# Routing three token tiles in one chain, and another order around the first experts

## The chip, the cores and the metric

One core of a Trainium2 chip runs the whole program. The metric is the device time of one execution in microseconds; lower is better. Engines are named as in the profile: PE (TensorE), DVE (VectorE), ACT (ScalarE), POOL (GpSimd) and SP, whose queue issues nearly all DMAs.

## The reference

One layer of a hybrid trunk for 128 context and 256 latent tokens, 384 in all, D = 1024, float32. Four token mixers and a merge come first and are not touched. Then comes the mixture of experts, of which this case is:

```python
h = modulated RMSNorm(x)                      # (384, 1024)
scores = sigmoid(h @ router_w)                # (384, 64)
biased = scores + router_bias
group score = sum of the two best of each of 8 groups of 8; keep the 4 best groups (ties: lower index)
chosen = the 8 best biased scores in those groups
gates = 2.5 * scores[chosen] / sum(scores[chosen])
y = shared: (silu(h @ sh_w1) * (h @ sh_w3)) @ sh_w2        # hidden width 256
  + sum over the chosen experts of gate * (silu(h @ w1[e]) * (h @ w3[e])) @ w2[e]
x = x + g2 * y;  output = RMSNorm(x) * final_g
```

## The kernel before

Tokens are three tiles of 128 (`t` = 0 to 2), matrices of activations are held with 128 rows in the partitions. PE writes into eight PSUM banks; a helper `Banks` hands them out in turn, and `open` waits until the last reader of a bank has freed it.

**Up to the experts** (PE's order, L1287 to L1329): router products of tiles 0 and 1, the shared expert's unit (0,0), router of tile 2, the transposes `turn_back(0)` and `turn_back(1)` of the normalised rows, unit (0,1), `turn_back(2)`, units (1,0) and (1,1). A unit is one half (f) of the hidden width, of `sh_w1` (i = 0) or `sh_w3` (i = 1). Then come the ranks of tokens within their expert, the transposed gates, the shared down products of tiles 0 and 1, the transposed places, and the down products of tile 2. They stay in banks 0 to 5, in which the experts' outputs are summed.

DVE runs a chain of some 25 instructions for each tile, from the scores to the gates (L2549 to L2571), nearly all of them waiting for the one before. Between the chains stands `low_parts(t)` (L2531), which makes the low part of the rows and frees the banks of `turn_back(t)`. `shared_hidden(f)` (L2538) multiplies the halves of the shared expert's hidden values. Then the places are worked out (L2580 to L2584).

**Experts.** A token row chosen by an expert takes one of 32 places of a quarter; four quarters form a pair (`a_` = 0 or 1) of up to 128 rows with weights of two experts, u = 0 and 1, in `w13[a_]` (4 MB) and `w2[a_]` (2 MB). Experts 0 to 3 come first without a plan ("first" pass); then a loop over q takes two pairs a turn ("mid"), and one more pair is "last". For one pair PE makes H (gate and up products, k = 0 to 7, L3076), HT (its transpose), and Y (down products, two halves, L3123), and adds Y to the sums (`scatter`, L2978).

Which experts fill the later pairs is worked out on the chip: DVE counts (`flag_counts`, L3287 to L3297), `pair_experts` and `place_quarters` (L3301 to L3337) alternate with small PE products, the plan steps X 0 and 1. X 2 to 4 make the tables of places, gates and expert numbers for the three tiles (`table`, L3342 to L3345). In the first pass these steps, the gathers G0 (rows of the first two pairs), the turned selections S0 and the gate rows B stand between the k's of H by the list `BETWEEN`; each has its bank by `FIRST_BANKS` (6 or 7), and DVE and ACT read the jobs in the list's order:

```python
BETWEEN = {(0, 0): ("X", 0, 0), (0, 1): ("G0", 0, 3), (0, 2): ("S0", 0, 0), (0, 3): ("X", 0, 1), (0, 4): ("S0", 1, 0),
           (0, 5): ("B", 0, 0), (0, 6): ("X", 0, 2), (1, 1): TURNS[0], (1, 2): TURNS[1], (1, 4): ("B", 0, 2), (1, 6): ("B", 0, 3)}
```

**SP's queue** (L2808, L3476 to L3493) issues in order: `w13[0]` as soon as the ring of earlier weights is free; behind unit (1,1) of the shared expert `w2[0]`, `w13[1]` and `w2[1]`; the stores of the three row sums that POOL makes (`token_rows`, the third waits for table X 2 and for the first store); the final gain; then, behind table X 2, `refill`: `w13[a_]` when H of that pair is filled, `w2[a_]` when its second Y is.

## Time and profile before

| | |
|---|---|
| median of 3 runs | 1371.96 us (1371.27 to 1373.4) |
| profiled execution | 1372.2 us, span 1370.3 us |
| PE busy | 1329.5 us, 97% |
| DVE busy | 602.4 us, 44% |
| ACT busy | 377.5 us, 28% |
| POOL busy | 306.8 us, 22% |
| moved by DMA | 321.57 MB, mean 235 GB/s |
| granted clock of PE | 0.995 of full |

Times are from the start of the span. A busy PE is not PE at its peak, since matmuls overlap. The part that is changed lies between 792 and 865 us; the loop over expert pairs fills the time from 875 to about 1341 us.

### The profile page before, as it was taken

How to read it: one execution, taken by the hardware profiler on the slowest of the kernel's cores; microseconds unless marked ns; L12 is line 12 of the kernel's file. 1: busy time of each engine (PE TensorE's matmuls, PEld its weight loads, DVE VectorE, ACT ScalarE, POOL GpSimd, SP SyncE). 2: the span in 40 equal slices, each digit the busy share in tenths (PEclk: the TensorE clock that was granted, in tenths of full speed). 3: DMA queues.
4: the chain of work that ended last, by engine and by line, in shares of the span. 5: the costliest groups of instructions: out<-in, count | busy, mean ns of one | idle time of the engine just before them, and what ended most of it. 6: DMA issues, size and time to landing. Idle time of an engine off the chain costs nothing.

```text
span 1370.3 us, 20640 instructions
## 1 busy us (share of the span) xinstructions
PE 1329.5 (97%) x7692; PEld 925.7 (68%) x7692; DVE 602.4 (44%) x1363; ACT 377.5 (28%) x764; POOL 306.8 (22%) x247
## 2 busy tenths in 40 slices
PE   7999999999999998999999999999999999999996
PEld 2694799989988997678988865444544444444452
DVE  3467442785644486363232375222233223222224
ACT  3222222222545245232411331211222122211122
POOL 0431234243235555234332010100000000000001
PEclk9999999999999999999999999999999999999998
DMA  9640433043313334457435347999999999999991
GB/s 362 218 115 21 138 93 123 14 141 93 93 62 93 108 111 152 156 195 168 128 123 168 106 181 272 418 418 421 420 420 421 420 420 420 420 420 419 419 414 81
DMA packets 109744, 321.57 MB, mean 235 GB/s; under 512 B 12489, under 2 KB 72649, under 8 KB 81136
## 3 DMA queue, kind: packets, MB, share of 16 engines
q1 hardware_dynamic: 98416, 307.68, 59.1%
q0 software_dynamic: 2560, 8.81, 1.6%
q10 hardware_dynamic: 8704, 4.20, 1.2%
q8 instruction: 44, 0.72, 0.2%
q14 instruction: 20, 0.16, 0.0%
HBM read 320.11 MB, written 4.33 MB: 237 GB/s over the span
## 4 chain that ended last, share of the span: by engine, by line
PE 85%; DMA 10%; DVE 2%; ACT 1%; issue 1%; SPq 0%; DVEq 0%
PE banks L686 24%; PE banks L653 17%; PE banks L3076 13%; DMA w<-in_exp_w 7%; PE banks L3123 7%; PE banks L2978 6%; PE banks L1093 2%; PE banks L2963 2%; PE banks L1263 2%; DMA ring<-in_ada_w 2%; PE banks L2971 1%; PE banks L737 1%; PE banks L926 1%; PE banks L660 1%; PE banks L805 1%
## 5 line engine op out<-in xcount | busy, mean ns | idle before, releaser
L3076 PE MATMUL banks<-w,xg 128*64 128x512 f32 (+1 forms) x1312 | 235.9, 594 | 2.0 <-DMA w<-in_exp_w 1.8
L3076 PEld LDWEIGHTS banks<-w,xg 128*64 128x64 f32 (+1 forms) x1312 | 72.0, 126 | 151.2 <-issue 126.0
L686 PE MATMUL banks<-hT,ring 128*128 128x192 f32 x888 | 156.0, 329 | 5.0 <-issue 4.8
L686 PEld LDWEIGHTS banks<-hT,ring 128*128 128x128 f32 x888 | 146.5, 191 | 8.9 <-issue 6.7
L3453 POOL DMA_INDIRECT fetched<-token_rows,row_of_place x32 | 32.2, 1006 | 443.4 <-DVE row_of_place L3254 433.3
L3123 PE MATMUL banks<-w,hidT 128*64 128x512 f32 (+1 forms) x656 | 122.6, 601 | 0.8 <-DMA w<-in_exp_w 0.6
L2978 PE MATMUL banks<-y,selT 128*128 128x512 f32 x384 | 114.9, 415 | 0.0
L686 PE MATMUL banks<-x,ring 128*128 128x192 f32 x592 | 109.1, 327 | 0.9 <-ACT late L1441 0.9
L686 PE MATMUL banks<-x,combos 128*128 128x192 f32 x592 | 108.4, 326 | 0.7 <-ACT late L1434 0.7
L686 PEld LDWEIGHTS banks<-x,ring 128*128 128x128 f32 x592 | 97.8, 191 | 3.1 <-issue 1.7
L686 PEld LDWEIGHTS banks<-x,combos 128*128 128x128 f32 x592 | 98.1, 190 | 1.2 <-POOL ring L2625 0.9
L3265 DVE SCALAR_TENSOR_TENSOR hid<-banks,gslot,sil 128x256 f32<-128x256 f32 x33 | 15.9, 483 | 178.6 <-ACT sil L3158 178.0
L2978 PEld LDWEIGHTS banks<-y,selT 128*128 128x128 f32 x384 | 66.3, 189 | 35.1 <-issue 26.2
L653 PE MATMUL banks<-yT,ring 128*128 128x384 f32 x256 | 86.7, 488 | 0.9 <-issue 0.9
L2625 POOL TENSOR_TENSOR ring<-ring,combos 128x512 f32<-128x512 f32 x37 | 49.6, 1341 | 168.3 <-PE banks L686 168.1
L3123 PEld LDWEIGHTS banks<-w,hidT 128*64 128x64 f32 (+1 forms) x656 | 32.0, 125 | 67.2 <-issue 46.1
L3274 DVE TENSOR_TENSOR y<-banks,y 128x512 fp32r<-128x512 f32 x66 | 45.7, 692 | 63.0 <-ACT y L3177 63.0
L3158 ACT ACTIVATE sil<-banks 128x256 f32<-128x256 f32 x33 | 12.7, 385 | 201.6 <-PE banks L3076 201.6
L653 PEld LDWEIGHTS banks<-yT,ring 128*128 128x128 f32 x256 | 47.5, 190 | 30.1 <-issue 1.9
L3177 ACT ACTIVATE y<-banks 128x512 fp32r<-128x512 f32 x66 | 39.4, 597 | 89.8 <-PE banks L3123 89.8
L2609 POOL TENSOR_TENSOR ring<-ring 128x512 f32<-128x512 f32 x37 | 52.7, 1424 | 45.5 <-DMA ring<-in_w_in 42.7
L2617 POOL TENSOR_TENSOR combos<-combos,ring 128x512 f32<-128x512 f32 x37 | 49.3, 1332 | 49.2 <-PE banks L686 48.0
(513 smaller groups left out, 1939.9 us busy)
## 6 DMA issues: line engine op xcount, KB each, us to landing
w<-in_exp_w SPq DMA_DIRECT2D x198, 1024.0 KB, 14.2
ring<-in_w_in SPq DMA_DIRECT2D x46, 1024.0 KB, 5.4
ring<-in_ada_w SPq DMA_DIRECT2D x24, 1024.0 KB, 7.0
ring<-in_w_branch SPq DMA_DIRECT2D x8, 1024.0 KB, 5.2
ring<-in_w_out SPq DMA_DIRECT2D x4, 1024.0 KB, 6.6
arena<-in_sh_w SPq DMA_DIRECT2D x3, 1024.0 KB, 8.2
x<-in_x_sample SPq DMA_DIRECT2D x4, 512.0 KB, 8.1
token_rows<-whole_rows SPq DMA_DIRECT2D x3, 384.0 KB, 21.9
```

The lines of the kernel that those rows point to most:

```text
L653: last = mm(out, lhsT=lhsT, rhs=rhs, start=i == 0, stop=i == len(pairs) - 1)
L686: last = mm(out, lhsT=w[:, k, :], rhs=tokens[:, k, :], start=start and k == 0, stop=k == KD // 2 - 1, skip_group_check=not start)
L1093: last = mm(ps[:, h * P:(h + 1) * P], lhsT=lhsT, rhs=rhs, start=True, stop=True)
L2609: s_combos.on(g.tensor_tensor(a21, a11, a21, ALU.subtract))
L2617: s_combos.on(g.tensor_tensor(combos[:, 0], combos[:, 1], a11, ALU.add))
L2625: s_combos.on(g.tensor_tensor(a11, a12, combos[:, 1], ALU.subtract))
L2978: ins = mm(psum[:, t * 2 + h, :], lhsT=selT[:, a_, t * P:(t + 1) * P], rhs=y[:, part, h * W:(h + 1) * W], start=False, stop=False)
L3076: ins = mm(ps[lo:hi, :], lhsT=xg[:, k, a_ * P + lo:a_ * P + hi], rhs=w13[:, a_, u, :, k, :], start=k == 0, stop=k == KD - 1)
L3123: ins = mm(ps[lo:hi, :], lhsT=hidT[:, f, lo:hi], rhs=w2[:, a_, u, f, h * W:(h + 1) * W], start=f == 0, stop=f == 1)
L3177: ins = on(y[:, HI, i * W:(i + 1) * W], ps, ACT.Copy)
L3274: ins = tt(y[:, LO, hh], ps, y[:, HI, hh].bitcast(F32), ALU.subtract)
L3453: nc.gpsimd.indirect_dma_start(fetched[:, a_, :], None, rows[:, :], bass.IndirectOffsetOnAxis(ap=row_of_place[:, 2 * a_:2 * a_ + 1], axis= ...
```

## The change

- **Routing.** The three chains become one with operands of 3 x 64 scores or 3 x 8 groups. The maxima, the top-8 searches and the replacements stay one for each tile or group, issued without a wait between them. `low_parts(0)` follows the gates, `low_parts(1)` the places, `low_parts(2)` comes between two calls in the experts' part (`middle`).
- **PE's order up to the experts.** Behind unit (0,1): ranks, transposed gates, `turn_back(2)`, transposed places; then units (1,0) and (1,1). Banks 6 and 7 are taken out of the turn for this.
- **The plan.** The steps X are no jobs any more. `step(i)` writes to bank 5 or 3 and counts on `s_steps`; DVE's tables count on `s_table`. Step 0 follows gather 0, step 1 follows k = 0 of H(0,0), step 2 follows k = 6, step 3 H itself, step 4 `down(0)`.
- **Shared down products.** `down(0)` stands behind step 3, `down(1)` and `down(2)` behind HT. `shared_hidden(1)` is behind `flag_counts` on DVE.
- **Gate rows B** all go into H(1,0). The staged selections lie in `g2row` in place of `y`, and some tiles have other addresses.
- **POOL and SP.** The third row sum waits for the first store alone. SP waits for the first table behind the third store, and the final gain comes behind the refill of pair 0. POOL's clearing of `fetched` waits for Y(0,0).

The diff, cut to its core:

```diff
+            def down(t):
+
+                for h in range(2):
+                    banks.settle(pe, t * 2 + h)
+                    for f in range(2):
+                        mm(psum[:, t * 2 + h, :], lhsT=hid[:, f, tok[t]], rhs=wsh_down[:, f, h * W:(h + 1) * W],
+                           start=f == 0, stop=False)
...
-            for f, i in ((0, 1), (1, 0), (1, 1)):
+            def shared_unit(f, i):
+
                 ps = banks.open(pe, ("shared", f, i), ("act", "dve")[i])
                 banks.close(shared_products(ps, f, i, 0, T))
-                if (f, i) == (0, 1):
-                    turn_back(2)
-
-
-            banks.settle(pe, 6)
-            pe.wait_ge(s_gates.sem, NT)
+
+            for p in (6, 7):
+                banks.settle(pe, p)
+                banks.held.add(p)
+            shared_unit(0, 1)
+            pe.wait_ge(s_gates.sem, 1)
             for t in range(NT):
                 pairs = [(sums[:, 3, :], chosen[:, t, :])] + [(sums[:, 4, :], chosen[:, u, :]) for u in range(t)]
                 last = contract(psum[:, 6, t * NE:(t + 1) * NE], pairs)
             last.then_inc(s_ranks.sem, 1)
-            banks.settle(pe, 7)
             for t in range(NT):
                 last = nc.tensor.transpose(psum[0:NE, 7, tok[t]], gates[:, t, 0:NE], ident[:, :])
             last.then_inc(s_rowsT.sem, 1)
-            banks.emptied(pe, ("shared", 1, 1))
-            w = wsh_down[:, :, :]
+            turn_back(2)
+            pe.wait_ge(s_placed.sem, 1)
             for t in range(NT):
-                for h in range(2):
-                    banks.settle(pe, t * 2 + h)
-                    for f in range(2):
-                        mm(psum[:, t * 2 + h, :], lhsT=hid[:, f, tok[t]], rhs=w[:, f, h * W:(h + 1) * W],
-                           start=f == 0, stop=False)
-                if t == 1:
-                    pe.wait_ge(s_placed.sem, 1)
-                    for u in range(NT):
-                        last = nc.tensor.transpose(psum[0:NE, 6, tok[u]], places[:, u, 0:NE], ident[:, :])
-                    last.then_inc(s_rowsT.sem, 1)
-            expert_work["tensor"](pe)
+                last = nc.tensor.transpose(psum[0:NE, 6, tok[t]], places[:, t, 0:NE], ident[:, :])
+            last.then_inc(s_rowsT.sem, 1)
+            shared_unit(1, 0)
+            shared_unit(1, 1)
+            for t in range(NT):
+                banks.emptied(pe, ("h2", t, 1))
+            for p in (3, 5):
+                banks.settle(pe, p)
+            expert_work["tensor"](pe, down, lambda: banks.emptied(pe, ("shared", 1, 1)))
...
+            scores3, chosen3 = pick[:, 0:NT, :], chosen[:, :, :]
+            biased, g8 = (part(20992 + i * NT * NE, NT * NE) for i in range(2))
+            gs, rank, keep, pen, top = (part(20672 + i * NT * NGRP, NT * NGRP) for i in range(5))
+            tot = part(20672 + 5 * NT * NGRP, NT)
+            cmp_, masked = (sq[:, i * NT * NE:(i + 1) * NT * NE] for i in range(2))
             for t in range(NT):
                 banks.emptied(dve, ("router", t))
-                scores = pick[:, t, :]
-                lane.link(tt(biased, scores, rbias, ALU.add))
-                for g in range(NGRP):
-                    lane.do(v.max(g8[:, g * 8:g * 8 + 8], biased[:, g * 8:g * 8 + 8]))
-                lane.wait_own()
-                lane.link(tt(gs, by8(g8)[:, :, 0], by8(g8)[:, :, 1], ALU.add))
-
-                mine, other = gs[:, :, None].to_broadcast([P, 8, 8]), gs[:, None, :].to_broadcast([P, 8, 8])
-                lane.link(tt(by8(cmp_), other, mine, ALU.is_equal))
-                lane.link(tt(cmp_, cmp_, before, ALU.mult))
-                lane.link(tt(by8(masked), other, mine, ALU.is_gt))
-                lane.link(tt(cmp_, cmp_, masked, ALU.add))
-                lane.link(v.reduce_sum(rank, by8(cmp_), axis=AX))
-                lane.link(ts(keep, rank, float(TOPG), None, ALU.is_lt))
-                lane.link(ts(pen, keep, -NEG, NEG, ALU.mult, ALU.add))
-                lane.link(tt(by8(masked), by8(biased), each(keep, NE), ALU.mult))
-                lane.link(tt(by8(masked), by8(masked), each(pen, NE), ALU.add))
-                lane.link(v.max(top, masked))
-                lane.link(v.match_replace(left, top, masked, TAKEN))
-                lane.link(ts(chosen[:, t, :], left, TAKEN / 2, None, ALU.is_lt))
-                lane.link(tt(cmp_, chosen[:, t, :], scores, ALU.mult))
-                lane.link(v.reduce_sum(tot[:, 0:1], cmp_, axis=AX))
-                lane.link(v.reciprocal(tot[:, 0:1], tot[:, 0:1]))
-                s_gates.on(ts(gates[:, t, 0:NE], cmp_, tot[:, 0:1], ROUTED, ALU.mult, ALU.mult))
-                dve.wait_ge(s_gates.sem, t + 1)
-                if t < 2:
-                    low_parts(t)
-            shared_hidden(0)
-            low_parts(2)
-            shared_hidden(1)
+            lane.link(tt(three(biased), scores3, over(rbias), ALU.add))
+            for g in range(NT * NGRP):
+                lane.do(v.max(g8[:, g * 8:g * 8 + 8], biased[:, g * 8:g * 8 + 8]))
+            lane.wait_own()
+            lane.link(tt(gs, by8(g8)[:, :, 0], by8(g8)[:, :, 1], ALU.add))
+
+            of_tile = lambda w: w.rearrange("p (t g) -> p t g", t=NT)
+            mine = of_tile(gs)[:, :, :, None].to_broadcast([P, NT, NGRP, NGRP])
+            other = of_tile(gs)[:, :, None, :].to_broadcast([P, NT, NGRP, NGRP])
+            four = lambda w: w.rearrange("p (t g e) -> p t g e", t=NT, g=NGRP)
+            lane.do(tt(four(masked), other, mine, ALU.is_gt))
+            lane.link(tt(four(cmp_), other, mine, ALU.is_equal))
+            lane.link(tt(three(cmp_), three(cmp_), over(before), ALU.mult))
+            lane.link(tt(cmp_, cmp_, masked, ALU.add))
+            lane.link(v.reduce_sum(rank, by8(cmp_), axis=AX))
+            lane.link(ts(keep, rank, float(TOPG), None, ALU.is_lt))
+            lane.do(ts(pen, keep, -NEG, NEG, ALU.mult, ALU.add))
+            lane.link(tt(by8(masked), by8(biased), each(keep, NT * NE), ALU.mult))
+            lane.link(tt(by8(masked), by8(masked), each(pen, NT * NE), ALU.add))
+            for t in range(NT):
+                lane.do(v.max(top[:, t * 8:t * 8 + 8], masked[:, t * NE:(t + 1) * NE]))
+            lane.wait_own()
+            for t in range(NT):
+                lane.do(v.match_replace(g8[:, t * NE:(t + 1) * NE], top[:, t * 8:t * 8 + 8], masked[:, t * NE:(t + 1) * NE], TAKEN))
+            lane.wait_own()
+            lane.link(ts(chosen3, three(g8), TAKEN / 2, None, ALU.is_lt))
+            lane.link(tt(three(cmp_), chosen3, scores3, ALU.mult))
+            lane.link(v.reduce_sum(tot, three(cmp_), axis=AX))
+            lane.link(v.reciprocal(tot, tot))
+            s_gates.on(stt(gates[:, :, 0:NE], three(cmp_), ROUTED, tot[:, :, None].to_broadcast([P, NT, NE]), ALU.mult, ALU.mult))
+            low_parts(0)
 
             dve.wait_ge(s_ranks.sem, 1)
-            lane.link(ts(places[:, :, 0:NE], chosen[:, :, :], -FAR, FAR, ALU.mult, ALU.add))
+            dve.wait_ge(s_gates.sem, 1)
+            lane.link(ts(places[:, :, 0:NE], chosen3, -FAR, FAR, ALU.mult, ALU.add))
             rank3 = psum[:, 6, 0:NT * NE].rearrange("p (t e) -> p t e", t=NT)
-            work3 = sq[:, 0:NT * NE].rearrange("p (t e) -> p t e", t=NT)
-            lane.link(tt(work3, chosen[:, :, :], rank3, ALU.mult))
-            s_placed.on(tt(places[:, :, 0:NE], places[:, :, 0:NE], work3, ALU.add))
+            lane.link(tt(three(cmp_), chosen3, rank3, ALU.mult))
+            s_placed.on(tt(places[:, :, 0:NE], places[:, :, 0:NE], three(cmp_), ALU.add))
             dve.wait_ge(s_placed.sem, 1)
-            expert_work["vector"](dve)
+            low_parts(1)
+
+            def middle():
+                shared_hidden(0)
+                low_parts(2)
+
+            expert_work["vector"](dve, middle, lambda: shared_hidden(1))
...
-    first_staged = y[:, :, :].rearrange("p i n -> p (i n)")[:, 0:2 * NT * TURN].rearrange("p (a t c) -> p a t c", a=2, t=NT)
+    first_staged = g2row[:, :, :].rearrange("p i n -> p (i n)")[:, 0:2 * NT * TURN].rearrange("p (a t c) -> p a t c", a=2, t=NT)
+    s_steps, s_table = sem("plan_steps_summed"), sem("plan_tables_ready")
...
-    FIRST_BANKS = {("G0", 0, 0): 6, ("G0", 0, 1): 7, ("G0", 0, 2): 6, ("X", 0, 0): 6, ("G0", 0, 3): 6, ("S0", 0, 0): 6,
-                   ("X", 0, 1): 6, ("S0", 1, 0): 6, ("B", 0, 0): 6, ("X", 0, 2): 6, ("H", 0, 0): 7, ("B", 0, 1): 6, ("HT", 0, 0): 7,
-                   ("X", 0, 3): 6, ("Y", 0, 0): 7, ("X", 0, 4): 6, ("Y", 0, 1): 7, ("S", 0, 0): 7, ("S", 1, 0): 7, ("B", 0, 2): 7,
-                   ("B", 0, 3): 7}
+    FIRST_BANKS = {("G0", 0, 0): 6, ("G0", 0, 1): 7, ("G0", 0, 2): 6, ("G0", 0, 3): 6, ("S0", 0, 0): 6, ("S0", 1, 0): 6,
+                   ("H", 0, 0): 7, ("HT", 0, 0): 7, ("Y", 0, 0): 6, ("Y", 0, 1): 7, ("S", 0, 0): 7, ("S", 1, 0): 7,
+                   ("B", 0, 0): 7, ("B", 0, 1): 7, ("B", 0, 2): 7, ("B", 0, 3): 7}
     JOBS_FIRST = list(FIRST_BANKS) + JOBS[6:]
-    BETWEEN = {(0, 0): ("X", 0, 0), (0, 1): ("G0", 0, 3), (0, 2): ("S0", 0, 0), (0, 3): ("X", 0, 1), (0, 4): ("S0", 1, 0),
-               (0, 5): ("B", 0, 0), (0, 6): ("X", 0, 2), (1, 1): TURNS[0], (1, 2): TURNS[1], (1, 4): ("B", 0, 2), (1, 6): ("B", 0, 3)}
+    BETWEEN = {(0, 1): ("G0", 0, 3), (0, 2): ("S0", 0, 0), (0, 4): ("S0", 1, 0), (1, 1): TURNS[0], (1, 2): TURNS[1],
+               (1, 3): ("B", 0, 0), (1, 4): ("B", 0, 1), (1, 5): ("B", 0, 2), (1, 6): ("B", 0, 3)}
+    STEP_BANKS = (5, 3, 5, 3, 5)
+    STEPS_IN_H = {0: 1, 6: 2}
...
+        def step(i):
+
+            if i == 4:
+                pe.wait_ge(s_table, 1)
+            plan_step(i, psum[:, STEP_BANKS[i], :]).then_inc(s_steps, 1)
...
                     add_job(("G0", 0, j))
+                    if j == 0:
+                        step(0)
...
+                    if first and a_ == 0 and k in STEPS_IN_H:
+                        step(STEPS_IN_H[k])
...
-                    add_job(("B", 0, 1))
+                    step(3)
+                    hidden_ready()
+                    down(0)
+                    step(4)
...
-                    add_job(("X", 0, 3))
+                    pe.wait_ge(s_table, 2)
+                    down(1)
+                    pe.wait_ge(s_table, NT)
+                    down(2)
...
-                    if first and (a_, h) == (0, 0):
-                        add_job(("X", 0, 4))
...
+                act.wait_ge(s_out.sem, 16 * 6)
...
+        def plan_step(i):
+
+            dve.wait_ge(s_steps, i + 1)
+            ps = psum[:, STEP_BANKS[i], :]
+            if i < 2:
+                link(v.tensor_copy(got[0:NE, :], ps[0:NE, 0:4]))
+                (pair_experts, place_quarters)[i]()
+            else:
+                table(ps, i - 2)
...
+        middle()
         dve.wait_ge(s_copied, 2)
         flag_counts()
+        last_hidden()
+        plan_step(0)
...
+                if first and job == ("G0", 0, 1):
+                    plan_step(1)
+                if first and job in (("G0", 0, 3), ("H", 0, 0)):
                     i = int(job[0] == "H")
+                    dve.wait_ge(s_out.sem, 16 * 6)
                     dve.wait_ge(s_read["act"], read(q, "act", ("S0", i, 0), kind))
                     keep_selection(i, first_staged[:, i, :, :].bitcast(F32)).then_inc(s_first, 1)
-                if job == ("X", 0, 4):
-                    dve.wait_ge(s_read["dve"], read(q, "dve", job, kind))
+                    if i == 0:
+                        plan_step(2)
+                    else:
+                        plan_step(3)
+                        plan_step(4)
+                if first and job == ("Y", 0, 0):
+                    dve.wait_ge(s_table, NT)
...
                 pool.wait_ge(s_stored0, 16)
-                pool.wait_ge(s_read["dve"], read(0, "dve", ("X", 0, 2), "first"))
             nc.gpsimd.tensor_tensor(whole_rows[:, t % 2, :], h2[HI][:, t, FROM_ROWS:].bitcast(F32), h2[LO][:, t, FROM_ROWS:].bitcast(F32),
                                     ALU.add).then_inc(s_whole, 1)
-        pool.wait_ge(s_filled, 1)
+        pool.wait_ge(s_filled, filled(0, ("Y", 0, 0), "first"))
...
-        sp.wait_ge(s_out.sem, 16 * 6)
-        sp.wait_ge(s_gq, 1)
-        sp.dma_start(fg_row[:, :], a["final_g"].rearrange("(a n) -> a n", a=1).to_broadcast([P, D])).then_inc(s_fg, 16)
-        sp.wait_ge(s_read["dve"], read(0, "dve", ("X", 0, 2), "first"))
+        sp.wait_ge(s_table, 1)
...
+        sp.dma_start(fg_row[:, :], a["final_g"].rearrange("(a n) -> a n", a=1).to_broadcast([P, D])).then_inc(s_fg, 16)
+        sp.wait_ge(s_table, NT)
```

## Rows read from the trace of the kernel before

**Rows 1.** Windows: us from the start, busy of each engine, granted clock, DMA share, GB/s.

```profile
798.00:800.00 2.00, 2.00 (x10) 1.33 (x9) 1.97 (x4) 1.98 (x3) 0.00 (x0) 1.00 0.00 0
840.00:848.00 8.00, 7.47 (x45) 4.52 (x43) 5.85 (x25) 1.94 (x4) 2.44 (x2) 1.00 0.02 6
1100.00:1200.00 100.00, 99.63 (x496) 47.35 (x496) 30.64 (x86) 20.19 (x40) 8.00 (x8) 1.00 1.01 420
```

**Rows 2.** Timeline of SP's queue: start, us, engine, line, what, count.

```profile
785.19 1.98 SPq L2808 DMA_DIRECT2D w<-in_exp_w  x4
814.74 0.80 SPq L3480 DMA_DIRECT2D w<-in_exp_w  x2
...
850.93 2.04 SPq L3476 DMA_DIRECT2D w<-in_exp_w  x4
...
864.98 1.92 SPq L3476 DMA_DIRECT2D w<-in_exp_w  x4
...
882.26 1.93 SPq L3476 DMA_DIRECT2D w<-in_exp_w  x4
...
912.99 2.15 SPq L3476 DMA_DIRECT2D w<-in_exp_w  x4
...
1316.72 1.84 SPq L3476 DMA_DIRECT2D w<-in_exp_w  x4
```

**Rows 3.** Landings of the four transfers into w13[1] issued from 864.98 on.

```profile
DMA to landing us min/median/max: 8.1/10.9/14.4
```

**Rows 4.** Timeline of PE, the first plan table.

```profile
842.80 0.34 PE L3011 MATMUL banks<-plan,late 64*1 64x24 f32 x4 [0.32 <-DVE plan L3337]
```

**Rows 5.** Timeline of ACT: third router, copies of the transposed blocks.

```profile
794.85 0.22 ACT L1347 ACTIVATE arena<-banks 128x64 f32<-128x64 f32 x1 [2.48 <-PE banks L653]
...
823.55 0.86 ACT L3182 ACTIVATE rowsE<-banks 64x384 f32<-64x384 f32 x2 [13.48 <-PE banks L1327]
```

**Rows 6.** Timeline of DVE, from the routing to the plan.

```profile
792.66 0.21 DVE L2549 TENSOR_TENSOR arena<-arena 128x64 f32<-128x64 f32 x1
792.91 0.64 DVE L2551 MAX8 arena<-arena 128x8 f32<-128x8 f32 x8
...
797.83 1.98 DVE L2531 TENSOR_TENSOR h_low<-banks,h_high 128x512 fp32r<-128x512 f32 x2
...
816.66 0.35 DVE L2583 TENSOR_TENSOR sq<-arena,banks 128x192 f32<-128x192 f32 x1
817.05 1.46 DVE L2584 TENSOR_TENSOR late<-late,sq 128x192 f32<-128x192 f32 x1
...
827.35 0.14 DVE L3297 TENSOR_SCALAR flags<-where 64x1 f32<-64x1 f32 x1
829.80 0.69 DVE L3267 COPY xg<-banks 128x512 f32<-128x512 f32 x1 [2.32 <-PE banks L2963]
...
837.97 0.15 DVE L3269 COPY got<-banks 64x4 f32<-64x4 f32 x1 [2.13 <-PE banks L3004]
...
842.38 0.27 DVE L3337 TENSOR_SCALAR plan<-plan 64x232 f32<-64x232 f32 x1
```

**Rows 7.** Chain that ended last: start, us, what.

```profile
796.57 6.95 PE banks L1263 x32
...
804.39 10.32 PE banks L1263 x32
814.71 1.28 PE banks L653 x12
...
833.50 1.61 PE banks L2963 x12
835.10 1.01 PE banks L3076 x4
```

**Rows 8.** Timeline of POOL, the first two row sums.

```profile
814.70 3.60 POOL L3442 TENSOR_TENSOR whole_rows<-h_high,h_low 128x768 f32<-128x768 f32 x2 [71.13 <-DVE h_low L2531]
```

**Rows 9.** The page's DMA issues: KB each, median us to landing.

```profile
token_rows<-whole_rows SPq DMA_DIRECT2D x3, 384.0 KB, 21.9
```

More of the change, by code:

```diff
@@ L2541, in _ @@
             dve.wait_ge(s_late.sem, 16 * N_LATE)
-            biased, g8, sm, before, rbias = (pick[:, i, :] for i in (3, 4, 5, 6, 7))
-            by8 = lambda w: w.rearrange("p (g e) -> p g e", g=NGRP)
-            gs, rank, keep, pen, top, tot = (sm[:, i * 8:i * 8 + 8] for i in range(6))
-            cmp_, masked, left = sq[:, 0:64], sq[:, 64:128], sq[:, 128:192]
+            before, rbias = pick[:, 6, :], pick[:, 7, :]
+            over = lambda w: w[:, None, :].to_broadcast([P, NT, NE])
+            three = lambda w: w.rearrange("p (t e) -> p t e", t=NT)
@@ L2830, in expert_tiles @@
         sb("row_sum", P, 2),
-        sb("flags", P, 8),
-        sb("where", P, 16),
-        sb("got", P, 4),
         sb("expert_of", P, 2, NX // 4, dt=mybir.dt.int32),
-        sb("pad", P, 206 - NX // 2),
+        sb("pad", P, 120),
         sb("w13", P, 2, 2, 2, KD, FE),
         sb("w2", P, 2, 2, 2, D),
-        sb("sel", P, NT, 8, QUARTER, dt=F32R),
-        sb("selT", P, 2, T, dt=F32R),
-        sb("y", P, 2, D, dt=F32R),
-        sb("quarter_places", P, NT, 8 + NX),
-        sb("quarter_gates", P, NT, 8 + NX),
-        sb("rounds", P, 2, dt=mybir.dt.int32),
         sb("rowsE", P, 2, T),
@@ L2847, in expert_tiles @@
         sb("plan", P, 4, NX),
+        sb("flags", P, 8),
+        sb("where", P, 16),
+        sb("got", P, 4),
+        sb("rounds", P, 2, dt=mybir.dt.int32),
+        sb("row_of_place", P, 4, dt=mybir.dt.int32),
+        sb("y", P, 2, D, dt=F32R),
+        sb("selT", P, 2, T, dt=F32R),
+        sb("sel", P, NT, 8, QUARTER, dt=F32R),
+        sb("quarter_places", P, NT, 8 + NX),
         sb("turn_by", P, NT, TURN, dt=F32R),
+        sb("quarter_gates", P, NT, 8 + NX),
         sb("fetched", P, 2, D - FROM_ROWS),
+        sb("final_gain", P, D),
         sb("g2row", P, 2, D),
-        sb("final_gain", P, D),
-        sb("row_of_place", P, 4, dt=mybir.dt.int32),
         sb("whole_rows", P, 2, D - FROM_ROWS),
@@ L2954, in count, with tensor_part @@
         return eng.value_load(rounds[0:1, i:i + 1], min_val=2 + i, max_val=NX // 8)
-    def tensor_part(pe):
+    def tensor_part(pe, down, hidden_ready):
         mm = nc.tensor.matmul
@@ L3046, in add_job @@
                 what, a_, i = job
-                if what == "X":
-                    close_bank(plan_step(i, open_bank(job)))
-                elif what == "B":
+                if what == "B":
                     close_bank(gate_row(i, open_bank(job)))
@@ L3267, in take @@
                 ins = v.tensor_copy(xg[:, 2 * i:2 * i + 2, :].rearrange("p k n -> p (k n)"), ps)
-            elif what == "X" and i < 2:
-                ins = v.tensor_copy(got[0:NE, :], ps[0:NE, 0:4])
-            elif what == "X":
-                ins = table(ps, i - 2)
             else:
@@ L3367, in body @@
                 take(q, job, kind)
-                if job[0] == "X" and job[2] < 2:
-                    dve.wait_ge(s_read["dve"], read(q, "dve", job, kind))
-                    (pair_experts, place_quarters)[job[2]]()
-                if first and job in (("X", 0, 1), ("H", 0, 0)):
+                if first and job == ("G0", 0, 1):
+                    plan_step(1)
+                if first and job in (("G0", 0, 3), ("H", 0, 0)):
                     i = int(job[0] == "H")
+                    dve.wait_ge(s_out.sem, 16 * 6)
                     dve.wait_ge(s_read["act"], read(q, "act", ("S0", i, 0), kind))
                     keep_selection(i, first_staged[:, i, :, :].bitcast(F32)).then_inc(s_first, 1)
-                if job == ("X", 0, 4):
-                    dve.wait_ge(s_read["dve"], read(q, "dve", job, kind))
+                    if i == 0:
[5 more added lines that the diff above has]
+                    dve.wait_ge(s_table, NT)
                     select_tokens(slice(8, 16))
@@ L3505, in sync_part @@
         refill(0, 0, slice(0, 1), "first")
-        sp.wait_ge(s_read["dve"], read(0, "dve", ("X", 0, 4), "first"))
+        sp.dma_start(fg_row[:, :], a["final_g"].rearrange("(a n) -> a n", a=1).to_broadcast([P, D])).then_inc(s_fg, 16)
+        sp.wait_ge(s_table, NT)
         n2 = count(sp, 1)
```

7 lines of the change are left out of this document (4 added, 3 removed).

## The prediction

> **What bounds the kernel now.** I read the windows first. Up to 840 us the TensorE is busy all the time and the DMA engines come and go; from 851 on both are full. In [rows 1] the reader is to see three states: no transfer at all at 798 to 800, 0.02 of the DMA engines between 840 and 848, and 1.01 at 420 GB/s in the expert loop, with the TensorE busy for 99.63 of 100 us. Two resources run side by side there, so the second view is the sync engine's timeline, which dates each refill of the expert weights. A refill of w13[0] leaves at 882.26 and the next at 912.99 [rows 2]: 30.73 us for one turn, which is the TensorE's own pace. Fourteen turns at that pace would end at 882.26 + 430.2 = 1312.5; the fifteenth refill leaves at 1316.72, so 4.2 us were lost on the way to late weights. The third view confirms it: of the four transfers issued from 864.98 on, the last leaves 1.4 us later and lands 14.4 us after that, at 880.8 [rows 3].
>
> So the transfers are a little slower per turn than the TensorE. They fall behind turn by turn, and late in the loop they set the pace. The end follows from when the chain of transfers gets going near 865 to 881, and the TensorE has 4.2 us to spare. This is the ruler for the change: **what counts is when H(1,0) of the first pass is filled (it lets the refill of w13[1] leave) and how late the queue then is.** What happens before matters through these two alone.
>
> **The change, part by part.** Both versions have the same TensorE work between 796.57 and the end of H(1,0) (nothing is added or left out, plan steps and gate rows included), so I compare only the stalls. Before, one of 0.32 us shows at the first plan table [rows 4] and I estimate as much again where the chain passes through ACT and DVE: 0.6 together.
>
> *Routing in one chain.* It can't start before the third router's scores are out: ACT starts that sigmoid at 794.85 and needs 0.22, so 795.1, where the old chain for tile 0 starts at 792.66 [rows 5, 6]. That chain takes 5.17 us, to 797.83 where low_parts begins [rows 6]. A 192-wide operation with a PSUM operand takes 0.35 and the next starts 0.39 after it; 64-wide ones are 0.25 apart [rows 6]. Some 12 wide steps each get 0.14 dearer: +1.7. Eight maxima took 0.64 us [rows 6]; 24 at the same slope take some 1.75: +1.1. Three top-8 searches and three replacements for one of each: +0.8. Two steps no longer wait: -0.4. The sum is 8.35 us (lower bound 6.3, if width cost nothing; upper bound 15.5, three whole chains), nearest to the wide row. Gates stand at 795.2 + 8.35 = 803.5. The TensorE ends shared(0,1) at 796.57 + 6.95 = 803.5 [rows 7]. They meet, with no slack.
>
> *Ranks, places, transposes ahead of shared(1,0).* From the gates on, DVE does low_parts(0), 1.98 [rows 6], then the three place steps (0.33 + 0.39 + 0.39 by the wide row), then the first half of low_parts(1), 1.0, which frees the bank that shared(1,0) wants: with signals 4.3 us, so 807.85. The TensorE has 2.8 us of work in that time (ranks 1.28 [rows 7], nine small transposes, turn_back). **Stall: 1.5.** It is DVE's chain that sets 807.85, so each microsecond that the routing takes more goes straight into it. The two remaining shared units take 10.32 [rows 7] and end at 818.2.
>
> *Row copies, flags, step 0.* ACT copies the two transposed blocks in 0.86 [rows 5] behind the silu of shared(1,0), done by 814.5, against 824.4 before. DVE is at low_parts(2) until 814.5 too. Then the flags: 824.41 to 827.49, 3.1 us [rows 5, 6], so 817.6 if nothing disturbs them; the TensorE wants them after gather 0, at 818.2 + 1.4 = 819.6. But low_parts(2) also releases GpSimd's two row sums, 3.60 us at 814.70 [rows 8], and these now lie on the flags, no longer on the place steps. In the old run a 192-wide operation with two SBUF operands beside them took 1.46 us, ending at 818.51, right after the sums, while its neighbour with a PSUM operand took 0.35 [rows 6]. I read this as held until the sum beside it ended. Held so, the first flag steps wait for both sums, and the last 2.1 us come after 818.2: 820.3. The bounds are 817.6 (free) and 820.7. Step 0 then ends at 820.65, pair_experts (2.05) at 823.0, the copy of gather 1 (0.69, [rows 6]) at 823.75; without stalls the TensorE would be there at 822.7. **Stall: 1.1.**
>
> The Trainium skill (SBUF, State Buffer, the passage on the shared pair of ports) says that GpSimd and a VectorE instruction with two SBUF inputs or in a two-port mode lock each other out for the whole instruction. The old trace alone could also be read as a mere stretch of 1.1 us; by that, flags would be out at 818.7 and this stall would be 0.2, by the skill's rule it is the 1.1 taken here. No row shows a flag step beside a GpSimd sum.
>
> *Step 1 behind k=0, and S0.* After the copy of gather 1: one k (1.01), step 1 (0.33), got and place_quarters on DVE (837.97 to 842.65, 4.7, [rows 6]), the copy of gather 3 (0.69), signals: 6.9 us until the bank is free for S0(0). The copy of gather 3 stands behind place_quarters in DVE's order. Meanwhile the TensorE has k=0, step 1, k=1, gather 3 (at most 1.61) and k=2: 4.8 us [rows 7]. **Stall: 2.1**, and nothing hides it. In the old order place_quarters ran beside k=4, S0(1), k=5, a gate row and k=6.
>
> *The rest of H(0,0), shared down products, steps 3 and 4.* Tables come out 3 to 7 us before the down products behind which they are wanted end; no stall. Their cover is the 3.4 us of each down(t). The four gate rows move behind Y(0,1), into H(1,0): the same work, later, so Y(0,1) doesn't slip by more than 2.1 less than H(1,0).
>
> Sum of stalls 1.5 + 1.1 + 2.1 = 4.7, less the old 0.6: **H(1,0) is filled 4.1 us later**, and the refill of w13[1] leaves at 864.98 + 4.1 = 869.1 [rows 2].
>
> *The sync queue.* First loads wait for shared(1,1): 818.2 instead of 814.74 [rows 2], and take some 4 us to issue. The first row stores are queued behind their 8 MB; they landed 22 us after their own issue [rows 9], so now near 844. GpSimd's third sum waits for that, SP's third store waits for the sum (1.8), and the refill stands behind that store in SP's order: about 848.2 instead of 850.93 [rows 2]. So SP's new wait on the first table is idle, and the queue gains 2.7 us; the final gain's 0.5 MB now come behind this refill (1.3 us). The old last landing of w13[1] was 880.8 [rows 3]; by the queue alone it would be 879.8.
>
> *What H(1,0) lets go.* An undisturbed w13 block of 4 MB: issued at 785.19, nothing moves any more at 798 [rows 1, 2], so at most 12.8 us. Issue at 869.1 + 12.8 = 881.9, later than the queue's 879.8. **The transfer chain is 1.1 us later than before**, and the TensorE, 4.1 late with 4.2 to spare, just fits. All that follows is unchanged. The profiled execution took 1372.2 us (span 1370.3), so 1373.3; the median of the runs shown lies 0.2 lower: 1373.1.
>
> **Rivals.**
> 1. *Slower, the routing chain is longer than its cover.* Speaks for it: the chain decides at zero slack, and 4-dimensional operands of 192 elements have no row. Each microsecond adds one to H(1,0) and to the transfers, and past 0.1 us the TensorE's spare is gone as well. From 10 us for the chain on (1.65 more), the result is 1.1 + 1.65 = +2.75, outside 0.2%. A second GpSimd collision would do the same. Up to 1376.
> 2. *The stalls are small.* If the flags are not held and the chain has 1 us less, H(1,0) is 2 us later, 867.0 + 12.8 = 879.8: the queue's own bound. Then -1.0: 1371.0. This is also the floor. Even with no stall at all the queue alone can't give more.
> 3. *The transfers were locked to H(1,0) one to one,* that is, no lateness is absorbed: +4.1, 1376. Against it: the last landing took 14.4 from the last of four issues, 15.8 from the first, and an undisturbed block 12.8.
> 4. *The refill leaves early, as SP's wait on the table would allow* (about 839), and the queue never runs dry. Then w13[0] and w2[0] are done 5 us sooner, but w13[1] still can't leave before H(1,0). With H(1,0) where the forecast has it the time stays 1373.1. Only with the TensorE early as well could the gain pass 2.7 us.
>
> **Numbers.** Forecast with its neighbourhood (+0.2 to +2.7): 0.45. Rival 2, with all of 4 that stays inside: 0.27. Rival 1: 0.15, rival 3: 0.06. More than 0.2% faster: 0.07, for what I don't see. 0.2% is 2.7 us and about what a measurement of this kernel can tell from no change. Same: 0.72, slower: 0.21. The likeliest case alone spans 1372.0 to 1374.8; with the floor and most of rival 1 the range is 1370.8 to 1376.0.
>
> **What the new profile would show.** Gates at 803.5 (late by what rival 1 takes); a gap of the TensorE of about 1.5 us ahead of shared(1,0); flag steps of over 1 us beside GpSimd's sums; a gap of 2 us ahead of S0(0) released by the copy of gather 3; DMA engines idle from 843 to 848 and again just before 869; refill of w13[1] at 869, with its last landing at 882. The forecast is wrong if H(1,0) is filled at 865 or earlier, or if w13[1] lands later than its issue plus 13.

## The result and the profile after

| | before | changed |
|---|---|---|
| median (13 runs each) | 1371.27 us (1370.53 to 1373.4) | 1375.74 us (1374.74 to 1377.0) |
| profiled execution | 1372.2, span 1370.3 | 1374.9, span 1373.1 |

The ratio is 1.003, interval 1.0022 to 1.0038: the changed kernel is slower by 0.3%. Run again beside other kernels it gave 1375.09 against 1371.94 us, ratio 1.002 (1.0011 to 1.0029). The forecast was 1373.1, with no change as the likeliest verdict. The time lies inside the range by luck: its upper end, 1376.0, was there for rival 1, a longer routing chain, which did not come. The rise is 4.5 and 3.2 us where 1.1 was forecast, on the side of rival 3, which had 0.06.

The timeline of PE (the TensorE) in the changed kernel, the rows with a wait between 803 and 838 us. The number in brackets is the wait, behind it stands what ended it. Where [rows 4] had one wait of 0.32, there are three, 2.99 us together:

```profile
807.15 10.59 PE L1271 MATMUL banks<-hT,arena 128*128 128x384 f32 x32 [0.54 <-DVE h_low L2537]
...
819.71 0.27 PE L3019 MATMUL banks<-flags,sums 64*64 64x2 f32 x2 [0.56 <-DVE flags L3325]
...
829.91 0.53 PE L3009 MATMUL banks<-turn_by,sel 128*128 128x146 f32 x3 [1.89 <-DVE xg L3299]
```

The timeline of DVE, for [rows 6]: the long chain's last step, the low parts of tile 1, two flag steps and the copy of gather 3.

```profile
802.85 0.36 DVE L2588 SCALAR_TENSOR_TENSOR late<-sq,arena 128x192 f32<-128x192 f32 x1
...
806.08 1.97 DVE L2537 TENSOR_TENSOR h_low<-banks,h_high 128x512 fp32r<-128x512 f32 x2
...
814.07 1.66 DVE L3316 TENSOR_SCALAR farther<-rowsE,where 64x384 f32<-64x384 f32 x1
815.76 1.84 DVE L3317 TENSOR_SCALAR sq<-farther 64x384 f32<-64x384 f32 x1
...
829.10 0.67 DVE L3299 COPY xg<-banks 128x512 f32<-128x512 f32 x1
```

The first two row sums on POOL, for [rows 8], lie beside those flag steps:

```profile
813.70 3.68 POOL L3487 TENSOR_TENSOR whole_rows<-h_high,h_low 128x768 f32<-128x768 f32 x2 [70.31 <-DVE h_low L2537]
```

SP's queue, for [rows 2]. The first refill of w13[0] leaves 5.0 us earlier than before, that of w13[1] 3.1 later, and every refill of w13 in the loop 2.5 to 3.0 later, to the last one:

```profile
785.01 2.06 SPq L2826 DMA_DIRECT2D w<-in_exp_w  x4
...
845.91 3.10 SPq L3521 DMA_DIRECT2D w<-in_exp_w  x4
...
868.10 2.02 SPq L3521 DMA_DIRECT2D w<-in_exp_w  x4
...
885.19 2.07 SPq L3521 DMA_DIRECT2D w<-in_exp_w  x4
...
1319.49 1.80 SPq L3521 DMA_DIRECT2D w<-in_exp_w  x4
```

Windows, for [rows 1]: the transfers do start earlier (0.50 instead of 0.02 at 840 to 848), and then run dry just ahead of the refill at 868:

```profile
840.00:848.00 8.00, 8.00 (x27) 4.00 (x27) 1.15 (x5) 0.38 (x1) 1.80 (x1) 1.00 0.50 170
866.00:870.00 4.00, 4.00 (x24) 2.87 (x24) 0.48 (x1) 1.22 (x3) 0.00 (x0) 1.00 0.27 52
```

Windows around the first refill of the loop (882.26 before, 885.19 changed), the kernel before and then the changed one. Before, the transfers are full up to that refill. In the changed kernel they have run out of work just ahead of it (0.77; from 885 to 886 alone it is 0.14):

```profile
882.00:886.00 4.00, 4.00 (x28) 3.39 (x28) 1.11 (x5) 1.22 (x3) 0.00 (x1) 1.00 0.99 410
```

```profile
882.00:886.00 4.00, 4.00 (x33) 1.55 (x26) 0.44 (x1) 0.39 (x1) 0.00 (x0) 1.00 0.77 315
```

What PE waited for from 1150 to 1330 us (line, releaser, us in total, times, longest), changed kernel and then the kernel before. Between 890 and 1150 neither has a wait for the weights.

```profile
PE banks L3102 <- DMA w<-in_exp_w: 2.0, 3, 0.7
PE banks L3157 <- DMA w<-in_exp_w: 0.6, 2, 0.3
```

```profile
PE banks L3076 <- DMA w<-in_exp_w: 1.8, 3, 0.8
PE banks L3123 <- DMA w<-in_exp_w: 0.6, 2, 0.3
```

This is the pair to look at. If waits of the TensorE had taken up the 3 us, they would have shrunk. They are 2.6 and 2.4 us: all of the lateness is still there at the end.

### The profile page after: what moved, and what is told of

Its sections match the earlier page's. It is cut to its first block, busy times and chain, and to the rows that moved or that the text cites. A ratio compares the mean times of both kernels' runs of the same rounds, so it can differ in the third digit from the quotient of the medians.

```text
span 1373.1 us, 20615 instructions
## 1 busy us (share of the span) xinstructions
PE 1330.4 (97%) x7692; PEld 925.7 (67%) x7692; DVE 598.3 (44%) x1331; ACT 377.3 (27%) x764; POOL 306.6 (22%) x247
## 4 chain that ended last, share of the span: by engine, by line
PE 85%; DMA 8%; DVE 3%; ACT 1%; issue 1%; SPq 0%; DVEq 0%
PE banks L686 24%; PE banks L653 17%; PE banks L3102 13%; PE banks L3157 7%; DMA w<-in_exp_w 6%; PE banks L2998 6%; PE banks L1093 2%; PE banks L2983 2%; DMA ring<-in_ada_w 1%; PE banks L2991 1%; PE banks L737 1%; PE banks L926 1%; PE banks L805 1%; PE banks L660 1%; PE banks L1265 1%
## 5 line engine op out<-in xcount | busy, mean ns | idle before, releaser
L3189 ACT ACTIVATE sil<-banks 128x256 f32<-128x256 f32 x33 | 12.7, 385 | 201.9 <-PE banks L3102 201.9
```

## The experiments

The first load of w13[0] falls up to 2.7 us apart from execution to execution, before any of the work in question. So I measure from it. "H(1,0)" is the refill of w13[1] in the first pass, which leaves when H(1,0) is filled. "Arrival" is the refill of w13[0] in the loop's first turn, which leaves when the TensorE has filled the H of that pair. "Rest" is the end of the span less the arrival. Time and ratio are of the timed runs, the other columns of one profiled execution of each.

| kernel | time, beside before | ratio (interval) | H(1,0) | arrival | rest |
|---|---|---|---|---|---|
| before | | | 79.8 | 97.1 | 488.0 |
| changed | 1375.74, 1371.27 | 1.0030 (1.0022 to 1.0038) | 83.1 | 100.2 | 487.9 |
| changed, again | 1375.09, 1371.94 | 1.0020 (1.0011 to 1.0029) | 84.7 | 101.8 | 487.7 |
| gather first | 1372.06, 1371.70 | 1.0001 (0.9992 to 1.0010) | 81.1 | 98.2 | 487.8 |
| sums later | 1373.44, 1371.70 | 1.0011 (1.0002 to 1.0020) | 82.5 | 99.6 | 487.6 |
| gate rows late | 1374.40, 1371.70 | 1.0020 (1.0010 to 1.0029) | 81.1 | 101.7 | 487.7 |
| before, late H(1,0) | 1374.51, 1371.70 | 1.0023 (1.0014 to 1.0032) | 82.5 | 99.8 | 488.0 |
| both stalls | 1371.76, 1371.94 | 1.0001 (0.9992 to 1.0010) | 80.6 | 97.7 | 487.5 |
| places later | 1371.60, 1371.94 | 0.9995 (0.9986 to 1.0004) | 79.9 | 97.0 | 487.9 |
| queue part alone | 1378.45, 1371.94 | 1.0044 (1.0030 to 1.0058) | 88.3 | 105.6 | 487.7 |
| queue part, clean | 1371.41, 1371.58 | 1.0001 (0.9992 to 1.0010) | 79.8 | 97.1 | 487.3 |
| routing alone | 1371.59, 1371.58 | 1.0006 (0.9997 to 1.0015) | 80.1 | 97.2 | 488.1 |
| less ahead | 1370.72, 1371.58 | 0.9996 (0.9987 to 1.0005) | 78.5 | 96.1 | 488.1 |
| gap filled | 1374.29, 1371.58 | 1.0024 (1.0015 to 1.0033) | 83.0 | 100.1 | 487.4 |

Over arrivals 9.5 us apart the rest stays within 0.8 us. Inside these 0.8 us there is an order: the four kernels with the old order of the sync queue (before, late H(1,0), routing alone, less ahead) have 488.0 to 488.1, the ten with the new one 487.3 to 487.9. The new order may so be worth some 0.4 us behind the arrival; no median shows that.

**Gather first.** In the changed kernel, DVE does plan_step(1), with its place_quarters, behind the copy of gather 3:

```diff
-                if first and job == ("G0", 0, 1):
+                if first and job == ("G0", 0, 3):
```

> The changed kernel with one step moved on DVE: the copy of gather 3 stands ahead of place_quarters, so S0(0) finds its bank free. The gap of 1.89 us ahead of S0(0) should be gone and H(1,0) be filled at 866.0 instead of 867.9. Theory A (the end follows from when the refill of w13[1] leaves, the TensorE has some 4 us to spare) expects 1.9 us less than the changed kernel, as that refill leaves 1.9 earlier. Theory B (the TensorE's own lateness goes to the end one to one) expects the same 1.9. A rival that the difference to the kernel before lies in the loop (other tile addresses, slower transfers per turn) expects less than 1 us from it.

1372.06 us. The wait ahead of S0(0) is gone and the arrival is 2.0 us earlier than in the changed kernel.

**Sums later.** In the changed kernel, POOL's first sum stands behind the second plan step:

```diff
+        pool.wait_ge(s_plan, 2)
```

> The changed kernel with GpSimd's first row sums held back until the plan is worked out, so that they no longer lie beside the flags. If the two operands in SBUF of the sums hold the flag steps, L3316 and L3317 take 0.4 us each and not 1.7 and 1.8, the flags are out near 817.0 and not 819.6, and H(1,0) is filled 0.5 to 0.8 us earlier (the stall of 0.56 us ahead of step 0 and a part of the wait for gather 1's copy). Time: 0.5 to 0.8 us less than the changed kernel. If the flag steps are slow for another reason, nothing changes. The stores of the rows go out 8 us later, behind the same queue; if they were what holds the refill of w13[0], it leaves later, and the time does not change by it.

1373.44 us. The same two flag steps on DVE:

```profile
813.69 0.41 DVE L3316 TENSOR_SCALAR farther<-rowsE,where 64x384 f32<-64x384 f32 x1
814.14 0.35 DVE L3317 TENSOR_SCALAR sq<-farther 64x384 f32<-64x384 f32 x1
```

0.41 and 0.35 instead of 1.66 and 1.84: beside a GpSimd sum they were held. The flags come 2.7 us earlier, but they had cost the TensorE only its 0.56, which is gone (arrival 0.6 earlier). The wait ahead of S0(0) stays, 1.83.

**Gate rows late**, and **before, late H(1,0)**: two kernels that pull apart "when H(1,0) is filled" and "how much work stands ahead of the loop". The first is the changed kernel with three of its four gate rows behind H(1,0); the second the kernel before with one gate row made four times in H(1,0).

```diff
-               (1, 3): ("B", 0, 0), (1, 4): ("B", 0, 1), (1, 5): ("B", 0, 2), (1, 6): ("B", 0, 3)}
+               (1, 3): ("B", 0, 0)}
...
+                if first and a_:
+                    gate_row(1, psum[:, 7, :]).then_inc(s_late_row, 1)
...
+                        gate_row(2, psum[:, 7, :]).then_inc(s_late_row, 1)
+                        gate_row(3, psum[:, 7, :]).then_inc(s_late_row, 1)
```

> The changed kernel with three of the four gate rows moved from within H(1,0) to behind it: the same TensorE work up to the loop, but H(1,0) is filled 3.1 us earlier (864.8) and the refill of w13[1] leaves as early as before the change. The TensorE itself reaches the loop as late as in the changed kernel, or up to 1 us later, as one bank is shared. Theory A expects the time of the kernel before or up to 1 us less (3.5 to 5 us under the changed kernel). Theory B expects the changed kernel's time or 0.7 more.

```diff
-                    close_bank(gate_row(i, open_bank(job)))
+                    out = open_bank(job)
+                    for _ in range(4 if i == 2 else 1):
+                        ins = gate_row(i, out)
+                    close_bank(ins)
```

> The kernel before, in which one gate row within H(1,0) is made four times over (three times 1.04 us of TensorE work added, nothing else). H(1,0) is filled 3.1 us later, with the refill of w13[0] and the plan where they were. Theory A as I predicted it, with 2.2 us of lateness absorbed by the queue, expects 0 to +1.0 us over the kernel before. Theory B expects +3.1. If +3.1 to +4.5 comes out, the whole loss of the change is the lateness of H(1,0).

1374.4 and 1374.51 us. The fair partner of the first is the second profile of the changed kernel, since both show the half clock told of below: H(1,0) is filled 3.6 us earlier, w13[1] is on its way earlier, and the arrival is the same (101.7 and 101.8). So is the end. (It has a wait of its own of 0.7 us, for a gate row's bank.) The second, with 2.7 us more before the loop, ends 2.6 later and has none of the change's waits. The refill of w13[1] isn't the ruler; the arrival at the loop is. "Gate rows late" sets the two apart with this refill early. No kernel has it late with the TensorE on time, so it isn't shown that a late queue costs nothing.

**Changed, again**, for its profile:

> The changed kernel once more, beside the next three on one chip. In the traces so far, counted from the first load of w13[0], the end is later than in the kernel before by 3.0 us here, 0.9 with gather 3 first, 2.1 with the sums later, 4.3 with late gate rows and 2.6 with the late H(1,0) of the old kernel; the refill of w13[0] in the first turn of the loop is later by 3.1, 1.2, 2.5, 4.7 and 2.7. So the new theory C is that the end follows the TensorE's arrival at the loop one to one. It expects 3 us over the kernel before.

1375.09 us. Its arrival is 1.6 later than in the first profile, though its waits are no longer (0.54, 0.56, 1.83). Windows right behind the last of them (the granted clock stands ahead of the DMA share):

```profile
830.00:833.00 3.00, 3.00 (x11) 1.09 (x9) 0.84 (x3) 0.35 (x1) 0.00 (x0) 0.50 1.00 421
```

0.50 of full is 1.2 GHz, the lower level. It lasts 3.4 us, from 829.7 on (0.85 at 829 to 830, 0.84 as the mean of 830 to 840). Four profiled executions have a TensorE wait of 1.8 to 1.9 us at this place. This one and that of "gate rows late" have the half clock behind it; the first profile of the changed kernel and "sums later" don't.

**Both stalls** joins the first two edits, and **places later** adds to it low_parts(1) ahead of the places on DVE and the transposed places behind shared(1,0) on PE:

```diff
+            shared_unit(1, 0)
...
-            shared_unit(1, 0)
...
+            low_parts(1)
...
-            low_parts(1)
```

> The changed kernel with both corrections, the copy of gather 3 ahead of place_quarters and GpSimd's sums behind the plan. The arrival at the loop should be 1.9 + 0.6 = 2.5 us earlier than in the changed kernel, 0.6 later than in the kernel before. Theory C expects +0.6 us over the kernel before, not distinguishable from it. If the order of the change had a gain of its own hidden by the stalls (the transfers' idle time at 840 to 848 us is cut by 3 us), the time falls below the kernel before.

> As with both corrections, and low_parts(1) ahead of the places on DVE, with the transposed places behind shared(1,0) on the TensorE. The waits ahead of shared(1,0) (0.3 and 0.54 us) should shrink to 0.3 or less, so the arrival at the loop is 0.5 earlier than with both corrections, that is at the kernel before's. Theory C expects 0.0 to +0.3 us over the kernel before.

1371.76 and 1371.6 us. Each edit takes off its own wait: arrival 100.2, 97.7, 97.0, where the kernel before has 97.1. The last is also the best version of the change, and can't be told from the kernel before.

**Queue part alone.** The kernel before, where GpSimd's third sum waits no longer for table X 2 and the final gain stands behind the refill:

```diff
-                pool.wait_ge(s_read["dve"], read(0, "dve", ("X", 0, 2), "first"))
...
-        sp.dma_start(fg_row[:, :], a["final_g"].rearrange("(a n) -> a n", a=1).to_broadcast([P, D])).then_inc(s_fg, 16)
...
+        sp.dma_start(fg_row[:, :], a["final_g"].rearrange("(a n) -> a n", a=1).to_broadcast([P, D])).then_inc(s_fg, 16)
```

> The kernel before with the part for GpSimd and SP alone: the third row sum no longer waits for the first table, and the final gain is issued behind the refill of pair 0. The refill of w13[0] should leave at about 847 instead of 850.9. If the idle time of the transfers were what costs, 1.5 to 3 us less. Theory C expects no change (within 0.5 us), since the arrival at the loop stays.

1378.45 us, the slowest of all, where the arrival theory expected no change. POOL, DVE and PE at that place, and the windows behind:

```profile
839.44 1.82 POOL L3441 TENSOR_TENSOR whole_rows<-h_high,h_low 128x768 f32<-128x768 f32 x1 [22.37 <-DMA token_rows<-whole_rows]
841.20 1.38 POOL L3444 MEMSET fetched<- 128x1536 f32 x1
```

```profile
839.51 3.20 DVE L3332 TENSOR_SCALAR plan<-late,where 64x232 f32<-64x232 f32 x1
842.74 0.33 DVE L3333 TENSOR_SCALAR plan<-plan,where 64x232 f32<-64x232 f32 x1
```

```profile
844.38 0.34 PE L3011 MATMUL banks<-plan,late 64*1 64x24 f32 x4 [3.18 <-DVE plan L3337]
```

```profile
840.00:850.00 10.00, 6.82 (x24) 3.41 (x24) 6.29 (x15) 0.98 (x2) 2.58 (x2) 0.70 0.10 39
850.00:860.00 10.00, 9.77 (x38) 5.35 (x39) 3.26 (x14) 1.47 (x3) 0.00 (x0) 0.62 0.93 361
```

A step of place_quarters takes 3.20 us instead of its neighbour's 0.33: it starts 0.07 behind the sum's start and ends 0.1 behind the memset. The TensorE waits 3.18, and then runs at half clock for 13.7 us from 843.9. Half of 13.7 is 6.9; 3.18 + 6.9 is 10.1 at the most, and the arrival is 8.5 later. The clock falls 0.5 us before the wait ends. The wait for the table, which seemed idle in the kernel before, kept a GpSimd sum off this chain.

**Queue part, clean**: the same, with the third sum behind the second plan step.

```diff
-                pool.wait_ge(s_read["dve"], read(0, "dve", ("X", 0, 2), "first"))
+                pool.wait_ge(s_plan, 2)
```

> The kernel before with the sync queue's part alone, but the third row sum of GpSimd placed behind the second plan step, away from place_quarters: the second half of the refills leaves earlier (w13[0] near 846 to 850 instead of 850.9) and the final gain's load stands behind it. Arrival theory: no difference, 0 within 0.5 us, as the refill of w13[0] in the loop stays at 97.1 us after the first load. Theory of the prediction: DMA queue gains up to 2.7 us, and the time 0 to 1.0 us lower. If GpSimd's memset of the fetched rows now meets a VectorE step with two SBUF inputs, that step takes over 1 us and the time is 0.5 to 2 us higher.

1371.41 us. The first refill of w13[0] leaves 62.1 us after the first load instead of 65.7, and no gain shows: arrival 97.1, ratio 1.0001 (0.9992 to 1.0010). The step of place_quarters takes 0.33 us again.

**Routing alone**: the one chain for all tiles in the kernel before, with the low parts of tiles 0 and 1 behind it and all else in its old place.

```diff
-            pe.wait_ge(s_gates.sem, NT)
+            pe.wait_ge(s_gates.sem, 1)
...
-                for g in range(NGRP):
+            for g in range(NT * NGRP):
```

> The kernel before with the routing of all tiles in one chain and nothing else; the plan steps, the gate rows and the sync queue stay where they were. Both theories put the gates near 803, and the TensorE, which has two shared units left between router products and the first plan table, should see a wait of at most 0.6 us ahead of shared(1,0) and none of the 1.9 us gap ahead of S0(0). Theory of the arrival (the end follows the TensorE's arrival at the expert loop one to one): the refill of w13[0] in the loop's first turn comes 97.1 to 97.7 us after the first load of w13[0], the time is within +0.0 to +0.6 of the kernel before. Theory that the long chain itself is the cost: arrival 2 to 3 us later and 1374 to 1375.

1371.59 us, no wait of the TensorE ahead of shared(1,0), arrival 0.1 later. The long chain by itself costs nothing here, where the ranks and places stand far behind it.

**Less ahead**: the kernel before without three quarters of the latent half's gate rows, which its result needs; it serves for its time alone.

```diff
-            for j in range(4):
+            for j in range(4 if i < 2 else 1):
```

> The kernel before with the gate rows of the latent half cut to one block of four, which leaves three quarters of those gate rows out: 1.5 us of TensorE work less in H(1,0), in front of the refill of w13[1]. Arrival theory: refill of w13[0] in the loop 95.5 us after the first load of w13[0] instead of 97.1, time 1.5 us lower, 1370.4 if before stands at 1371.9. Theory of the prediction (a queue that can be no earlier than about 1 us before the old time): 1.0 lower at the most, and the rest shows as waits of the TensorE for w13 in the loop. Theory that the transfers started near 846 are the bound: no difference.

1370.72 us. H(1,0) 1.3 earlier, arrival 1.0 (1.5 expected), the median 0.9 lower. The interval (0.9987 to 1.0005) doesn't tell this from no change, so it only fits with one to one on the early side, and doesn't exclude a floor of 1.0. Its first refill of w13[0] also leaves 0.8 earlier (64.9 us after the first load, not 65.7).

**Gap filled**: the changed kernel with fourteen small products in the wait ahead of S0(0).

```diff
+                    if first and (a_, k) == (0, 2):
+                        fill_gap(psum[:, STEP_BANKS[0], :])
```

> The changed kernel with fourteen small products, whose result nobody reads, in the gap of 1.9 us ahead of S0(0); the wait for the copy of gather 3 stays, only the TensorE is not idle in it. If the gap only costs its length, the time is that of the changed kernel (+0.0 to +0.5 for what the products run over the gap). If in some executions the gap also lets the granted clock fall to half for 3.4 us, then the windows of 820 to 850 show a granted clock of 0.98 or more in this run, the arrival is 100.2 us or less after the first load (not 101.8), and the median is 0.3 to 1.6 us below the changed kernel's 1375.1 to 1375.7.

1374.29 us. The profile shows 1.00 at 830 to 833 and the arrival of the first profile, as expected if only the clock is kept. But the ratio, 1.0024 (1.0015 to 1.0033), doesn't part from the changed kernel's two. How much of the changed kernel's median is clock stays open.

## Why the prediction was right and wrong

**Right: where the waits come.** Gates 803.2 (803.5 foretold; the chain took 8.2 us, 8.35 foretold), flags held by GpSimd's sums (out at 819.7, foretold 820.3), the wait ahead of S0(0) by the copy of gather 3 (1.89, foretold 2.1), the refill of w13[1] at 868.1 (869.1), with its last landing at 882.2 (881.9). That landing is 12.7 us behind the last of the four issues but 14.1 behind the first, from which the sum counted its 12.8, so the sign "later than its issue plus 13" depends on the issue meant. Its windows were right too (DMA idle just before that refill), but the transfers before it started 2.3 us earlier than foretold.

**Right, and now seen: flag steps held by GpSimd's sums.** The flag steps ran 1.66 and 1.84 beside the sums and 0.41 and 0.35 away from them. By the Trainium skill (SBUF — State Buffer, SBUF: two separate sides), where GpSimd meets a VectorE instruction with two SBUF inputs or in a two-port mode, the one that starts second is blocked until the first is done. The trace agrees: the two sums, 3.68 from 813.70 on, end at about 815.54 and 817.38 (if they are equally long), and the two steps at 815.73 and 817.60, each 0.2 behind. The second step has one input in SBUF (sq<-farther), so of the two kinds only the two-port mode fits it; no row shows a mode.

**Too large: two terms.** The stall ahead of shared(1,0) was 1.5 in the sum and 0.54 in the trace, since the TensorE had more to do there (it is busy for 3.38 of the 4.00 us from 803.2 on, not 2.8) and DVE freed the bank 0.7 earlier. That at the flags was 1.1 and is 0.56. H(1,0) is 3.3 us later, measured from the first load, not 4.1. The waits seen explain 2.7 us (2.99 less 0.32) of the 3.1 at the arrival; the other 0.4 stay open. A slip besides: the queue's own bound of 879.8, on which rival 2's floor rests, doesn't follow from its terms (880.8 - 2.7 + 1.3 = 879.4).

**The step that failed** is the one behind that sum: "The transfer chain is 1.1 us later than before, and the TensorE, 4.1 late with 4.2 to spare, just fits." Of 3.1 us at the arrival next to nothing was absorbed. Two parts of it were wrong.

First, I took the last landing of w13[1] (880.8 in the kernel before) as the start of the chain of transfers that sets the end. Counted from the first load, that landing is at 95.6 us before, 97.2 in the changed kernel, 95.0 in "gate rows late", 93.6 in "places later" and 95.6 in "less ahead". The end, counted likewise, moves by +3.0, +4.3, -0.3 and -0.9 us. It does not go by this landing. It goes by the arrival: +3.1, +4.7, -0.1 and -1.0.

Second, I took the 4.2 us that are lost late in the loop as spare for a TensorE that is late at its start. But a buffer is refilled when its H is done. In the changed kernel the transfers had run out of work when the arrival's refill left, as the windows show, and from 890 on they are full again (1.01 in the 100 us up to 990). I read the rows so: when the TensorE is late at the loop, each refill is as late, the transfers start their full stretch as late, and the same waits come on top. From the first refill of w13[0] in the loop to the fifteenth it was 434.5 us before [rows 2] and is 434.3 now. Rival 3, lateness passed on one to one, had 0.06; with the 3.1 us of the arrival it gives 1371.27 + 3.1 = 1374.4 beside the measured 1375.74, and 1371.94 + 3.1 = 1375.0 beside 1375.09. What speaks for rival 3 is the column "rest"; what spoke against it (14.4 and 15.8 to the last landing) was about landings by which the end does not go.

**Not foreseen: the clock.** Behind the wait of 1.8 to 1.9 us the granted clock fell to half for 3.4 us in two profiles, and in the second profile of the changed kernel the arrival is 1.6 later than in the first. That could be the 1.3 us between 1374.4 and the measured 1375.74, but "gap filled" didn't show it in the median. It is argued, not shown.

**Why no gain at all?** The change's corrected form gives the old time because it moves work, and leaves the TensorE's work ahead of the loop as it was. In the kernel before the TensorE is busy for 59.47 of the 60 us from 800 on: 0.5 us is all that there was to win in this stretch; what the change brought instead were three waits of its own. Two of them have one cause: a step that had run under cover was put in front of one that the TensorE needs sooner (the places ahead of low_parts(1), place_quarters ahead of the copy of gather 3). The third is the flags beside GpSimd's sums.

## What to carry to other kernels

Where a loop refills its buffers as they are used, its end can be tied to the time at which the compute engine reaches it, as here to within 0.8 us; waits for data late in the loop are no spare for being late at its start. Test this with a kernel that adds known work ahead of the loop before you count on slack. And when a short chain on VectorE is moved, list what GpSimd does beside its new place, and which copies stand behind it in VectorE's own order.

## What the runs showed of the hardware

- VectorE steps beside GpSimd's sums took 1.66 and 1.84 us instead of 0.41 and 0.35, and ended 0.2 behind a sum. One of 0.33 us became 3.20: it lasted through a sum of 1.82 and a memset of 1.38 that started 1.7 us after it. That the memset held it too is read from the end times; no run has the one without the other.
- A TensorE idle for 1.8 to 1.9 us, busy before and behind, was followed by 3.4 us at 1.2 GHz in two of four executions. In one of 3.18 us the clock fell 0.5 us before its end and stayed at that level for 13.7 us, in windows in which the engine was 6.82 busy of 10 and then 9.77 of 10.
